# Seven-product FFN blocks: steps in the order P1 P2 P5 P6 P7 P4 P3, one more sum on GpSimd, one more copied partial product

## The reference, cut to what matters

```python
h = rmsnorm(x, g_ffn) @ w_up          # 1024 x 4096
y = jnp.square(jax.nn.relu(h)) @ w_down
x = x + y
```

## Time and profile before

| | |
|---|---|
| median of 3 runs | 1503.9 us |
| profiled execution, its span | 1504.5 us, 1502.7 us |
| TensorE busy | 1412.1 us, 94% |
| VectorE, ScalarE, GpSimd busy | 1020.5, 532.2, 602.2 us |
| the 8 blocks | from 802 to about 1490 us |
| one block in the middle | 84.1 us |

### The profile page before, as it was taken

How to read it: one execution, slowest core, us unless ns; L and a number is a source line. 1 busy time by engine, 2 the same in 40 slices (tenths; PEclk the granted TensorE clock), 3 DMA queues, 4 the chain that set the end, 5 groups by cost and what they waited for, 6 DMA issues and landing times.

```text
span 1502.7 us, 28686 instructions
## 1 busy us (share of the span) xinstructions
PE 1412.1 (94%) x11826; PEld 1242.5 (83%) x11826; DVE 1020.5 (68%) x1759; ACT 532.2 (35%) x917; POOL 602.2 (40%) x454
## 2 busy tenths in 40 slices
PE   6999999999999889898997999999999999999996
PEld 4989989999998566685777979797988989797984
DVE  6883655568852677664527895958687685958588
ACT  6342322322221567543313333332323333332324
POOL 2121221888710000002218572827456372827453
PEclk9999999999999999999999999999999999999998
DMA  7412103722206732297000322131303122131312
GB/s 210 169 42 61 29 15 62 111 67 75 63 8 216 278 120 71 101 384 258 29 3 29 114 67 104 56 114 41 108 23 128 43 87 84 56 115 43 114 32 116
DMA packets 109811, 144.59 MB, mean 96 GB/s; under 512 B 26738, under 2 KB 78774, under 8 KB 107762
## 3 DMA queue, kind: packets, MB, share of 16 engines
q1 hardware_dynamic: 107618, 138.04, 29.3%
q0 software_dynamic: 2064, 4.72, 0.8%
HBM read 126.31 MB, written 21.14 MB: 98 GB/s over the span
## 4 chain that ended last, share of the span: by engine, by line
PE 78%; DVE 11%; issue 6%; ACT 3%; POOL 1%; DMA 1%; SPq 0%; DVEq 0%; ACTq 0%; POOLq 0%
PE PS L343 7%; PE PS L344 7%; PE PS L345 7%; PE PS L2706 6%; PE PS L2708 6%; PE PS L2707 6%; PE PS L2745 5%; PE PS L2746 5%; PE PS L2747 5%; PE PS L1647 2%; PE PS L1668 2%; PE PS L1687 2%; PE PS L2199 2%; PE PS L2201 2%; PE PS L2200 2%
## 5 line engine op out<-in xcount | busy, mean ns | idle before, releaser
L2745 PE MATMUL PS<-R_wb,R_ua 128*128 128x512 f32 x448 | 178.0, 397 | 10.9 <-DVE R_ua L2951 8.8
L2973 DVE TENSOR_TENSOR R_x<-R_x,PS 128x512 f32<-128x512 f32 x256 | 161.5, 677 | 20.1 <-PE PS L2747 20.1
L2746 PE MATMUL PS<-R_wb,R_ua 128*128 128x512 f32 x448 | 174.7, 390 | 0.0
L2747 PE MATMUL PS<-R_wb,R_ua 128*128 128x512 f32 x448 | 174.6, 390 | 0.0
L2874 POOL TENSOR_TENSOR R_wb<-R_slot,R_wb 128x1024 fp32r<-128x1024 f32 x56 | 146.0, 2607 | 42.0 <-ACT R_wb L2782 42.0
L2623 DVE TENSOR_TENSOR R_wb<-R_slot,R_wb 128x1024 fp32r<-128x1024 f32 x56 | 83.2, 1486 | 98.0 <-ACT R_wb L2617 98.0
L604 POOL TENSOR_TENSOR R_w<-R_wstage,R_w 128x1024 fp32r<-128x1024 f32 x29 | 75.0, 2589 | 176.2 <-ACT R_w L599 176.2
L2782 ACT ACTIVATE R_wb<-R_slot 128x1024 fp32r<-128x1024 f32 x56 | 59.4, 1060 | 240.1 <-PE PS L2747 131.7
L343 PE MATMUL PS<-xn_high,R_w 128*128 128x352 f32 x384 | 125.9, 328 | 3.2 <-ACT R_hscr L733 2.0
L343 PE MATMUL PS<-R_w,xn_low 128*128 128x256 f32 x432 | 125.6, 291 | 0.0
L344 PE MATMUL PS<-xn_low,R_w 128*128 128x352 f32 x384 | 123.2, 321 | 2.2 <-issue 2.2
(11 more groups left out here) (441 smaller groups left out, 3848.3 us busy)
## 6 DMA issues: line engine op xcount, KB each, us to landing
R_slot<-in_w_up SPq DMA_DIRECT2D x32, 512.0 KB, 3.9
R_slot<-in_w_down SPq DMA_DIRECT2D x32, 512.0 KB, 3.3
R_t<-x_sums SPq DMA_DIRECT2D x7, 2112.0 KB, 7.7
R_wstage<-in_w_in SPq DMA_DIRECT2D x28, 512.0 KB, 4.2
R_cache<-in_cache_attn_v SPq DMA_DIRECT2D x56, 256.0 KB, 8.9
R_cache<-in_cache_attn_k SPq DMA_DIRECT2D x28, 256.0 KB, 5.8
R_cache<-in_cache_attn_k SPq DMA_DIRECT2D x7, 1024.0 KB, 9.7
...
```

Of the source, the lines that this page charges most:

```text
L2745: pe.matmul(out, ul[:, f, ts], wh[:, f, :], start=(f == 0 and k in OPENS), stop=False, skip_group_check=True)
L2746: pe.matmul(out, uh[:, f, ts], wl[:, f, :], start=False, stop=False, skip_group_check=True)
L2747: mm = pe.matmul(out, uh[:, f, ts], wh[:, f, :], start=False, stop=(f == 1), skip_group_check=True)
L2973: ins = dve.tensor_tensor(part, part, PS[:, product_bank(k, p), :], ALU.add)
```

## The change

The steps of both parts come in the order P1 P2 P5 P6 P7 P4 P3. The quarter sums are formed another way, so that each uses the one before: S1 = a21 + a22 first, then S3, S2, S4. Of the four sums of squared quarters VectorE keeps one (S1 = q21 + q22, into `s1`), and GpSimd makes three (S3, S2 and S4, in place). In the up part P5 is copied by ScalarE as a fourth `kept` product, and VectorE adds P7 into it. `sample_product` moves ahead of the last unit of the last up step. The input's T sums follow the same scheme, T1 first; T1's parts get a tile of their own and T2 and T4 other places. The weight slots rotate accordingly.

```diff
-        P1, P2, P6, P7, P4, P5, P3 = STEPS = range(7)
+        P1, P2, P5, P6, P7, P4, P3 = STEPS = range(7)
...
-        XS1, XS2, XS3, XS4 = x12, x11, x22, x21
+        XS1, XS2, XS3, XS4 = x12, x22, x11, x21
...
-        UP_WEIGHT = {P1: "a11", P2: "a12", P6: "sa", P7: "a11", P4: "a22", P5: "a21", P3: "a12"}
+        UP_WEIGHT = {P1: "a11", P2: "a12", P5: "sa", P6: "a21", P7: "a11", P4: "a22", P3: "a12"}
...
-        LEFT = {P1: q11, P2: q12, P6: s2, P7: q21, P5: q11, P3: q12, P4: q22}
+        LEFT = {P1: q11, P2: q12, P5: s1, P6: q11, P7: q21, P4: q22, P3: q12}
...
-        KEPT, KEPT_AS = (P1, P6, P7), {P1: u11, P6: u12, P7: u22}
-        SUMMED, SUMMED_AS = (P2, P4, P5, P3), {P2: (u11, u11), P4: (u21, u22), P5: (u22, u22), P3: (u12, u12)}
-        SQUARED = ("u11", "u21", "u22", "u12 early", "u12 late")
+        KEPT, KEPT_AS = (P1, P5, P6, P7), {P1: u11, P5: u22, P6: u12, P7: u21}
+        SUMMED, SUMMED_AS = (P2, P7, P4, P3), {P2: u11, P7: u22, P4: u21, P3: u12}
+        SQUARED = ("u11", "u22", "u21", "u12 early", "u12 late")
...
+                    if k == P3 and p == 3:
+                        sample_product(b)
...
-                sample_product(b)
...
+                quarter_in(pool, b, "a21")
+                quarter_in(pool, b, "a22")
+                if b:
+                    pool.wait_ge(right_split, 7 * b)
+                pool.tensor_tensor(sa, a21, a22, ALU.add).then_inc(pool_sums, 1)
...
-                pool.tensor_tensor(a21, a21, a22, ALU.add).then_inc(pool_sums, 1)
...
                 right_low_part(b, P2)
+                pool.wait_ge(u_added, sum_count(b))
+                pool.tensor_tensor(q21, q11, q21, ALU.subtract).then_inc(pool_sums, 1)
+                right_low_part(b, P5)
+                pool.wait_ge(pool_sums, sums_count(b, H_S3))
+                pool.tensor_tensor(q11, q22, q21, ALU.subtract).then_inc(pool_sums, 1)
                 right_low_part(b, P6)
                 pool.tensor_tensor(w12, w22, w12, ALU.subtract).then_inc(pool_sums, 1)
                 right_low_part(b, P7)
-                pool.wait_ge(pool_sums, sums_count(b, W_T2))
-                pool.wait_ge(right_split, 7 * b + P2 + 1)
                 pool.tensor_tensor(w21, w21, w11, ALU.subtract).then_inc(pool_sums, 1)
                 right_low_part(b, P4)
-                pool.wait_ge(u_added, difference_count(b, "S2"))
                 pool.wait_ge(left_split, 7 * b + P2 + 1)
-                pool.tensor_tensor(q11, q11, s2, ALU.add).then_inc(pool_sums, 1)
-                right_low_part(b, P5)
-                pool.tensor_tensor(q12, q12, s2, ALU.subtract).then_inc(pool_sums, 1)
+                pool.tensor_tensor(q12, q12, q11, ALU.subtract).then_inc(pool_sums, 1)
                 right_low_part(b, P3)
...
-                dve.tensor_tensor(q21, q11, q21, ALU.subtract).then_inc(u_added, 1)
-                dve.wait_ge(u_added, difference_count(b, "S3"))
-                dve.tensor_tensor(s2, q22, q21, ALU.subtract).then_inc(u_added, 1)
+                dve.tensor_tensor(s1, q21, q22, ALU.add).then_inc(u_added, 1)
```

More of the change, by code:

```diff
@@ L2428, in x_taken @@
             j = F2_ORDER[q]
-            for kk in (range(2) if q < 4 else (1, 0)):
+            for kk in range(2):
                 dve.wait_ge(xs2_T, 2 * q + kk + 1)
@@ L2593, in sums_count @@
         def sums_count(b, which):
-            return 10 * b + which + 1
+            return 11 * b + which + 1
         def weights_free(eng, b, n):
@@ L2848, in phase_g_act @@
                     tile_squares(NCH)
-                for k in (P6, P7, P4, P5, P3):
+                for k in (P5, P6, P7, P4, P3):
                     right_high_part(b, k)
                     left_high_part(b, k)
-                    if last and k == P5:
-                        roots(0)
+                if last:
+                    roots(0)
                 if not last:
@@ L2954, in summed @@
                 dve.wait_ge(u_psum, hidden_index(b, k, p) + 1)
-                dve.wait_ge(u_kept, kept_count(b, {P2: P1, P4: P7, P5: P7, P3: P6}[k], p))
-                dst, src = SUMMED_AS[k]
-                dve.tensor_tensor(unit(dst, p), unit(src, p), PS[:, product_bank(k, p), 0:TH // 2], ALU.add).then_inc(u_added, 1)
+                dve.wait_ge(u_kept, kept_count(b, {P2: P1, P7: P7, P4: P7, P3: P6}[k], p))
+                part = unit(SUMMED_AS[k], p)
+                dve.tensor_tensor(part, part, PS[:, product_bank(k, p), 0:TH // 2], ALU.add).then_inc(u_added, 1)
             def hidden_squared(b, which):
-                k, p = {"u11": (P2, 1), "u21": (P4, 3), "u22": (P5, 3), "u12 late": (P3, 3), "u12 early": (P3, 1)}[which]
+                k, p = {"u11": (P2, 1), "u22": (P7, 3), "u21": (P4, 3), "u12 late": (P3, 3), "u12 early": (P3, 1)}[which]
                 dve.wait_ge(u_added, summed_count(b, k, p))
@@ L2985, in phase_g_dve @@
                     x_taken(dve, 8)
+                    dve.wait_ge(f_taken, NTILE + through(8) - 1)
+                    dve.tensor_tensor(XS1[:, :, LATE], x12[:, :, LATE], x11[:, :, LATE], ALU.subtract).then_inc(norm_split, 1)
+                up_low_part(dve, b, P5)
+                if not b:
+                    dve.wait_ge(f_high, high_made("t1 late"))
+                    dve.tensor_tensor(t1l[:, :, LATE], XS1[:, :, LATE], t1h.bitcast(F32)[:, :, LATE], ALU.subtract).then_inc(norm_split, 1)
@@ L2992, in phase_g_dve @@
[L2992 removed]
+                    dve.tensor_tensor(XS2[:, :, LATE], x22[:, :, LATE], XS1[:, :, LATE], ALU.subtract).then_inc(norm_split, 1)
+                    dve.wait_ge(norm_split, low_made("T2"))
+                    dve.tensor_tensor(XS3[:, :, LATE], XS2[:, :, LATE], x11[:, :, LATE], ALU.subtract).then_inc(norm_split, 1)
+                for p in UNITS[P2]:
+                    summed(b, P2, p)
+                up_low_part(dve, b, P6)
+                if not b:
+                    dve.wait_ge(f_split, pooled((7, "T4")))
+                    dve.wait_ge(f_high, high_made("t2 early"))
+                    dve.tensor_tensor(t2l[:, :, EARLY], XS2[:, :, EARLY], t2h.bitcast(F32)[:, :, EARLY], ALU.subtract).then_inc(norm_split, 1)
+                    dve.wait_ge(f_split, pooled("T4"))
@@ L3003, in phase_g_dve @@
                 up_low_part(dve, b, P4)
-                if not b:
-                    dve.wait_ge(f_high, high_made("t1"))
-                    dve.tensor_tensor(t1l, XS1, t1h.bitcast(F32), ALU.subtract).then_inc(norm_split, 1)
-                up_low_part(dve, b, P5)
+                for p in UNITS[P7]:
+                    summed(b, P7, p)
+                up_low_part(dve, b, P3)
+                hidden_squared(b, "u22")
+                for p in (0, 1):
+                    summed(b, P4, p)
@@ L3031, in phase_g_dve @@
                 added(b, P2, 0)
+                left_low_part(b, P5)
+                for p in range(1, 4):
+                    added(b, P2, p)
+                added(b, P5, 0)
                 left_low_part(b, P6)
                 for p in range(1, 4):
-                    added(b, P2, p)
+                    added(b, P5, p)
                 added(b, P6, 0)
@@ L3052, in phase_g_dve @@
                     added(b, P4, p)
-                added(b, P5, 0)
-                left_low_part(b, P3)
-                for p in range(1, 4):
-                    added(b, P5, p)
                 if not last:
```

197 lines of the change are left out of this document (87 added, 110 removed).

## The result

The changed kernel takes 1522.6 us (median of 5 runs, 1519.1 to 1525.1); the kernel before, run beside it, 1503.7. The ratio is 1.0127, with a 95% interval of 1.0112 to 1.0143: slower, at 1.3 us from the forecast of 1521.3. The profiled execution took 1525.1 us, at a span of 1523.3; it is the longest of the five, so the two spans differ by 20.6 us where the medians differ by 18.9.

The account below looks back on a forecast made before the run. TensorE, busy 94% of the span, bounds the kernel, so only its waits can be won. Down parts 10.0, up parts 8.4, less 1.2 in block 0, give +17.2 us on 1504.5: 1521.7, put at 1521.3, range 1514 to 1527.

Parts of the forecast that it names:

- The lock: VectorE instructions with two SBUF operands and GpSimd's keep each other out; a GpSimd sum ends 2.26 us after VectorE's instruction.
- the third rival: Squares on VectorE do not wait for GpSimd, so the sample product is 0.6 late: 1507 us, chance 0.12.
- The down part: In each block's down part, GpSimd's longer chain delays operands, with 1.5 us waits ahead of P7 and P4: 1.25 longer.
- The walk: Instruction-by-instruction timing of GpSimd and VectorE from the sample product on, giving when each down step can start.
- the first rival: GpSimd keeps up, its chain ending 3.5 us earlier, and no down step waits: 1495 us, chance 0.12.
- One instruction more on GpSimd: The down part's term: GpSimd has 12 instructions from the sample product on, VectorE one fewer; 1.25 us a block longer.
- The end of the up part: Late squares put the sample product 2.05 us late in place of 0.93; 1.2 a block longer.
- Block 0: In the first block P5 can start earlier, P6 waits for T2's low part; the down part starts 1.2 us earlier.
- The sum: Over all blocks: 10.0 for down parts, 8.4 for up parts, less 1.2 in block 0, together +17.2 us.
- the second rival: TensorE's clock falls more often: 1526 us from block 0's wait, 1543 with a fall in each block; chance 0.07.
- The forecast's own last step: The profiled execution stands 0.6 us above the median, so the whole kernel's 1521.7 was put at 1521.3.

Follow-up runs that it names:

- e1: The changed kernel without GpSimd's sum S2, so its output differs from the reference's: 1518.1 us, ratio 1.0101 to the kernel before.
- e4: The changed kernel with the sums S3 and S2 on VectorE, directly behind S1: 1516.0 us, ratio 1.0085 to the kernel before.
- e5: e4 with the weight sums T3 and T4 a step earlier in GpSimd's order: 1505.4 us, ratio 1.0020 to the kernel before.
- e7: The changed kernel with GpSimd's weight sum T4 ahead of the low part of P7's weight: 1531.2 us, ratio 1.0185 to the kernel before.
- e11: The changed kernel with VectorE's left half of P1 behind the early square of u12: 1512.9 us, ratio 1.0067 to the kernel before.
- e2: The changed kernel with the sample product back behind the last up unit: 1523.5 us, ratio 1.0136 to the kernel before.
- e8: The changed kernel with P2's sums ahead of T2's and T3's late columns in block 0: 1526.2 us, ratio 1.0152 to the kernel before.

## Why the prediction was right, point by point

**The lock.** Right, in both directions. The Trainium skill (SBUF — State Buffer, "SBUF: two separate sides") says that of a VectorE instruction with two SBUF inputs and a GpSimd instruction that reads SBUF the one that starts first gets the ports they share for the whole instruction, and that the other is blocked; the trace agrees, with squares of 2.68 and 3.45 in place of 1.25. That squares do not wait, the third rival, is out.

**The down part.** The walk gave P5 to P3, counted from the block's first matmul (986.12), at 55.8, 61.5, 68.5, 75.4 and 81.1, and the next block at 86.55; they stand at 55.8, 61.5, 68.5, 75.4, 81.2 and 86.8. The waits ahead of P2 and P5 went and 1.5 each came ahead of P7 and P4 (said: 1.5). GpSimd does not keep up: the first rival is out.

Right in its sum, this step named its cause too narrowly. It put the loss under "One instruction more on GpSimd"; e1 and e4 took one and two away and won 0.8 a block each, and e5 won 1.3 more by order alone. What costs 1.5 at a time is the round trip between a left half and the next step's weight sum, which the step's own walk contains (from 68.4 to 75.4). Before, the same trip ran beside TensorE. P7's left half ended at 1127.11 and the weight sum behind it at 1129.36; P4's left half ended at 1134.08, 6.97 after P7's:

```profile
1131.86 2.22 DVE L2951 TENSOR_TENSOR R_ua<-R_u,R_ua 128x1024 fp32r<-128x1024 f32 x1
```

TensorE started P7 1.98 and P4 0.45 after its left half was there, so it waited for neither:

```profile
1129.09 0.39 PE L2745 MATMUL PS<-R_wb,R_ua 128*128 128x512 f32 x1
...
1134.53 0.39 PE L2745 MATMUL PS<-R_wb,R_ua 128*128 128x512 f32 x1
```

In the changed kernel P7's left half ends only 0.05 before TensorE starts P7, so the lead is gone and the trip counts in full. GpSimd now makes two sums of squared quarters ahead of P7's weight sum, and made none there before: without S2 P7's wait is 0.84 (e1), without both 0.1 (e4). P4's wait stays through that, and goes where its weight sum comes earlier (e5, and e7 with all twelve instructions). The 0.05 that the prediction read as GpSimd ending on time is no spare time: it is what lies between a left half's end and TensorE's start whenever TensorE waits for it, as at 1054.53 and 1054.58.

**The end of the up part.** Said: the sample product 2.05 late, at t = 41.45; it is 2.02 late, at 41.44. e11 removes 1.5 of it by moving one VectorE instruction, which shows the two held instructions as the cause; e2 shows that the product's new place is not: with the old one the block takes the same 86.7.

**Block 0: the size right, the place wrong.** The step said that P5 starts at 817.1, and that P6 waits until 827.3 for T2's low part. P5 started at 821.55, and P6 at 828.78 without a wait. The walk looked at T1's input alone and left out that P5 also needs P2's sums, which in block 0 stand on VectorE behind T2's and T3's late columns (820.30 above). T2's low part, which the step took for P6's limit, ended at 828.04, so that P6 could not have started much earlier, and the term came out: the down part of block 0 starts 0.85 earlier (857.51 against 858.36), where 1.2 was taken. Block 0 itself is 1.44 shorter up to there, since its first matmul came 0.59 later in this execution (802.61 against 802.02). That the size held although the wait ahead of P5 was missed is luck: P6's limit lay close enough behind to hide it. e8 gave P2's sums the better place, and the wait moved on to P6.

**The sum.** 18.3 for seven blocks (said: 17.15), -0.85 up to the down part of block 0 (said: -1.2), 3.1 from the last down part's start to the end (said: 1.25): 20.6, which is the difference of the spans. The last term holds some 1.6 us of slow clock behind a stop in the last block (last section), which the forecast gave to no step; of the second rival that is what came. The forecast's own last step is off by 0.2: 1521.7 less 0.6 is 1521.1, not 1521.3.
